# Loading the second experts' weights in 4-MB pairs of units instead of single 2-MB units

## The reference, cut to what matters

```python
def hierarchical_moe(h, w_group, b_group, w_router, b_router, w_gate, w_up, w_down):
    ...
    comb = (jax.nn.one_hot(g_idx[:, 0], N_GROUPS, dtype=jnp.float32)[:, :, None]
            * inner[:, None, :]).astype(h.dtype)
    y = jnp.zeros_like(t)
    for g in range(N_GROUPS):
        a = jnp.einsum('td,edf->tef', t, w_gate[g])
        b = jnp.einsum('td,edf->tef', t, w_up[g])
        hid = jax.nn.silu(a) * b * comb[:, g, :, None]
        y = y + jnp.einsum('tef,efd->td', hid, w_down[g])
    return y.reshape(bsz, seq, d)
```

## Time and profile before

| | |
|---|---|
| time, median of 3 runs (all) | 1499.01 us (1494.44, 1502.03, 1499.01) |
| the profiled execution: its time, its span | 1499.14 us, 1497.3 us |
| PE busy | 1427.2 us, 95% of the span |
| DVE, ACT, POOL busy | 838.1, 571.6, 33.0 us |
| DMA | 443.45 MB, mean 296 GB/s over the span |
| mean granted PE clock | 0.990 |

### The profile page before, as it was taken

One profiled execution on the slowest core, in us unless ns is written; L12 is line 12 of the kernel. 1 busy time (PEld: TensorE's weight loads), 2 busy tenths in 40 slices (PEclk: granted clock), 3 DMA queues, 4 the chain that ended last, 5 costly groups with the idle time before them and its releaser, 6 DMA issues.

```text
span 1497.3 us, 24233 instructions
## 1 busy us (share of the span) xinstructions
PE 1427.2 (95%) x10238; PEld 1004.0 (67%) x10238; DVE 838.1 (56%) x1362; ACT 571.6 (38%) x850; POOL 33.0 (2%) x34
## 2 busy tenths in 40 slices
PE   9999999999999999999899987999999999999897
PEld 9988879999988888873588436984443443443335
DVE  6777697899979679940589207772212112112118
ACT  5673246564543447730477005432111111110115
POOL 0000100000030000000000001000000000000001
PEclk9999999999999999999999999999999999999999
DMA  9441026454531239999999995599999999999991
GB/s 379 158 154 59 2 112 230 158 225 169 184 141 60 85 131 418 406 362 412 412 419 368 420 420 207 198 426 373 427 427 427 426 427 426 427 427 427 426 425 63
DMA packets 48354, 443.45 MB, mean 296 GB/s; under 512 B 6768, under 2 KB 7280, under 8 KB 17008
## 3 DMA queue, kind: packets, MB, share of 16 engines
q1 hardware_dynamic: 47088, 438.37, 72.0%
q10 hardware_dynamic: 1152, 3.46, 0.7%
HBM read 440.75 MB, written 1.05 MB: 295 GB/s over the span
## 4 chain that ended last, share of the span: by engine, by line
PE 73%; DVE 12%; DMA 9%; ACT 3%; issue 2%; PEldq 0%; DVEq 0%; ACTq 0%; SPq 0%; PEld 0%
PE psum L241 71%; DMA sb_spare<-moe_up 3%; DMA sb_work<-moe_up 3%; DMA sb_work<-moe_last 2%; DVE sb_ring_r L1339 2%; DMA sb_ring<-moe_last 1%; DVE sb_work L3100 1%; PE psum L2885 1%; DVE sb_work L1433 0%; DVE sb_ring_r L300 0%; DVE sb_ring_r L2211 0%; DMA sb_ring<-w_dense 0%; PE psum L2289 0%; DVE sb_work L1859 0%; DVE sb_work L1431 0%
## 5 line engine op out<-in xcount | busy, mean ns | idle before, releaser
L241 PE MATMUL psum<-sb_work 128*64 128x512 f32 (+12 forms) x3580 | 330.7, 343 | 21.4 <-DVE sb_work L3100 7.8
L241 PEld LDWEIGHTS psum<-sb_work 128*64 128x64 f32 (+5 forms) x3580 | 168.0, 144 | 159.1 <-issue 135.8
L241 PE MATMUL psum<-sb_ring,sb_work 128*64 128x512 f32 (+2 forms) x660 | 159.3, 600 | 12.0 <-DVE sb_work L3100 4.7
L241 PE MATMUL psum<-sb_xT_r,sb_ring_r 128*128 128x256 f32 x512 | 143.9, 283 | 0.0
L241 PE MATMUL psum<-sb_split 128*128 128x512 f32 (+1 forms) x398 | 128.6, 382 | 0.0
L241 PEld LDWEIGHTS psum<-sb_ring,sb_work 128*64 128x64 f32 (+1 forms) x660 | 51.4, 141 | 104.0 <-issue 97.9
L3098 DVE TENSOR_TENSOR sb_work<-sb_work,psum 128x512 f32<-128x512 f32 x16 | 11.0, 687 | 167.7 <-ACT sb_work L3010 167.7
L3010 ACT ACTIVATE sb_work<-psum 128x512 f32<-128x512 f32 x16 | 9.6, 598 | 240.2 <-PE psum L241 240.2
L241 PEld LDWEIGHTS psum<-sb_xT_r,sb_ring_r 128*128 128x128 f32 x512 | 98.1, 192 | 0.3
L3068 DVE SCALAR_TENSOR_TENSOR sb_out_even<-psum,sb_work,sb_out_even 128x512 fp32r<-128x512 f32 x32 | 22.6, 747 | 125.8 <-ACT sb_out_even L2996 125.8
L241 PE MATMUL psum<-sb_split,sb_lnp_r 128*128 128x512 f32 (+1 forms) x260 | 87.8, 376 | 4.1 <-DVE sb_ring_r L2211 3.7
(11 more groups left out here) (524 smaller groups left out, 2881.6 us busy)
## 6 DMA issues: line engine op xcount, KB each, us to landing
sb_work<-moe_up SPq DMA_DIRECT2D x33, 2048.0 KB, 25.9
sb_ring<-moe_wide SPq DMA_DIRECT2D x52, 1024.0 KB, 10.3
sb_ring<-w_dense SPq DMA_DIRECT2D x23, 2048.0 KB, 8.5
sb_work<-moe_wide SPq DMA_DIRECT2D x43, 1024.0 KB, 11.1
sb_ring<-moe_up SPq DMA_DIRECT2D x18, 2048.0 KB, 25.3
sb_work<-moe_down SPq DMA_DIRECT2D x17, 2048.0 KB, 24.1
sb_ring<-ffn_wide SPq DMA_DIRECT2D x14, 2048.0 KB, 7.4
sb_ring<-moe_down SPq DMA_DIRECT2D x9, 2048.0 KB, 25.3
```

What stands on the lines that cost most here:

```text
L241: return nc.tensor.matmul(o, lhsT, rhs, start=start, stop=stop, **kw)
```

## The change

Two units whose homes are neighbours are loaded by one DMA of 4 MB, 128 rows of 32 KB. Homes 0 and 1, 2 and 3, 4 and 5, 6 and 7 become four such pairs; homes 8 and 9 stay single. Ring slots are given to homes 6 to 8 anew, so that 6 and 7 are slots 0 and 1; home 8 is now the slot that comes free first. `work`'s end and `spare` get one name together, `late_homes`. A pair has one semaphore, PE waits on it for either unit, and SP loads a pair when PE has read the second unit that was in it. In DRAM two units of a pack now lie in one row.

```diff
+        with nc.sbuf_tensor("sb_below_late", [P, EXTRA_AT], F32), \
+                nc.sbuf_tensor("sb_late_homes", [P, 4 * UNIT], F32) as late_homes:
+            pass
...
-        M2_RING = {6: U_MOE2 - 3, 7: U_MOE2 - 2, 8: U_MOE2 - 1}
+        M2_RING = {i: next(u for u in range(U_MOE2 - RING, U_MOE2) if u % RING == i - 6) for i in (6, 7, 8)}
+        PAIRED = 8
...
+        def home2_pair(n):
+
+            i = n % HOMES2
+            if i < 4:
+                return late_homes[:, UNIT * i:UNIT * (i + 2)]
+            if i == 4:
+                return work[:, SPLIT_AT:SPLIT_AT + 2 * UNIT]
+            return ring[:, 0:2, :].rearrange("p a d -> p (a d)")
+
+        def home2_sem(n):
+
+            i = n % HOMES2
+            return i - i % 2 if i < PAIRED else i
...
-                pe.wait_ge(sem(f"home_loaded{n % HOMES2}"), 16 * (m1_home_loads(n % HOMES2) + n // HOMES2 + 1 + (n % HOMES2 == LAST_HOME)))
+                r = home2_sem(n)
+                pe.wait_ge(sem(f"home_loaded{r}"), 16 * (m1_home_loads(r) + n // HOMES2 + 1 + (r == LAST_HOME)))
...
-                src = I["moe2_up"][g, j] if j < UP_UNITS else I["moe2_down"][g, j - UP_UNITS]
+                src = I["moe2_up"][g, j // 2] if j < UP_UNITS else I["moe2_down"][g]
+                if n % HOMES2 < PAIRED:
+                    sp.dma_start(home2_pair(n), src).then_inc(sem(f"home_loaded{home2_sem(n)}"), 16)
+                    return
+                src = src[:, UNIT * (j % 2):UNIT * (j % 2) + UNIT]
...
-                for n in range(4):
+                for n in (0, 2):
                     pack_load(n)
...
-                released(M2_RING[6])
+                released(M2_RING[8])
+                pack_load(8)
+                sp.wait_ge(sem("x_split"), 8 + HALVES)
+                pack_load(4)
+                for n in (6, 7):
+                    released(M2_RING[n])
                 pack_load(6)
-                sp.wait_ge(sem("x_split"), 8 + HALVES)
-                for n in (4, 5):
-                    pack_load(n)
-                for n in (7, 8):
-                    released(M2_RING[n])
-                    pack_load(n)
...
                 for n in range(HOMES2, UNITS2):
-                    unit_read(n - HOMES2)
-                    pack_load(n)
+                    if n % HOMES2 >= PAIRED:
+                        unit_read(n - HOMES2)
+                        pack_load(n)
+                    elif n % 2 == 0:
+                        unit_read(n + 1 - HOMES2)
+                        pack_load(n)
```

More of the change, by code:

```diff
@@ L2765, in program @@
         M2_UNIT_STEP = [f"k{UP_K * i + UP_K - 1}" for i in range(UP_UNITS)] + [f"d{DOWN_C * i + DOWN_C - 1}" for i in range(DOWN_UNITS)]
-        M2_RING = {6: U_MOE2 - 3, 7: U_MOE2 - 2, 8: U_MOE2 - 1}
+        M2_RING = {i: next(u for u in range(U_MOE2 - RING, U_MOE2) if u % RING == i - 6) for i in (6, 7, 8)}
+        PAIRED = 8
         def home2(n):
             i = n % HOMES2
[L2771 to L2774, removed]
+            if i < 4:
+                return late_homes[:, UNIT * i:UNIT * (i + 1)]
             if i == LAST_HOME:
@@ L2779, in home2 @@
             return work[:, SPLIT_AT + UNIT * (i - 4):SPLIT_AT + UNIT * (i - 3)]
-        assert SPLIT_AT + 2 * UNIT <= EXTRA_AT and EXTRA_AT + 3 * UNIT <= WORK
+        assert SPLIT_AT + 2 * UNIT <= EXTRA_AT and EXTRA_AT + 3 * UNIT == WORK
+        def home2_pair(n):
+            i = n % HOMES2
+            if i < 4:
+                return late_homes[:, UNIT * i:UNIT * (i + 2)]
[5 more added lines that the diff above has]
+            return i - i % 2 if i < PAIRED else i
         def m2_pe_names(g):
@@ L3111, in program @@
         OVER_BLOCKS = (FF_BLOCKS, (FF2 // P,), (FF2 // P,))
+        OVER_LOADED = (48, 80, 80)
         OVER_FIRST = (SLOTS1, SLOTS2, SLOTS2 + P)
@@ L3145, in overflow_sync @@
                             for i in range(2):
-                                sp.dma_start(ring[:, i, :].rearrange("p (u r) -> p u r", u=UP_UNITS),
-                                             I["moe2_up"][g].rearrange("u d (e w r) -> d e w u r", e=PACK, w=2)[:, e, i])\
-                                    .then_inc(loaded, 16)
+                                for b in range(2):
+                                    sp.dma_start(ring[:, i, 2 * D * b:2 * D * (b + 1)].rearrange("p (u r) -> p u r", u=2),
+                                                 I["moe2_up"][g, b].rearrange("d (u e w r) -> d e w u r", u=2, e=PACK, w=2)[:, e, i])\
+                                        .then_inc(loaded, 16)
                             sp.dma_start(ring[:, 2, :].rearrange("p (u r) -> p u r", u=DOWN_UNITS),
-                                         I["moe2_down"][g].rearrange("u f (e r) -> f e u r", e=PACK)[:, e])\
+                                         I["moe2_down"][g].rearrange("f (u e r) -> f e u r", u=DOWN_UNITS, e=PACK)[:, e])\
                                 .then_inc(loaded, 16)
@@ L3174, in overflow_body_tensor @@
                     over_wait(pe, n, it, 3 + 6 * b)
-                    pe.wait_ge(sem(f"over_loaded{n}"), it * (48 * nb) + 48 * (b + 1))
+                    pe.wait_ge(sem(f"over_loaded{n}"), it * (OVER_LOADED[n] * nb) + OVER_LOADED[n] * (b + 1))
                     w1, w3 = (ring[:, i, 0:DC * nch * P].rearrange("p (k n) -> p k n", k=DC) for i in range(2))
@@ L4086, in layouts @@
     A["moe2_up"] = gate_up.reshape(PACKS, PACK, UP_UNITS, UP_K, P, 2, FF2).transpose(0, 2, 4, 1, 5, 3, 6)\
-        .reshape(PACKS, UP_UNITS, P, -1)
-    A["moe2_down"] = inp["w_down_2"][0].reshape(PACKS, PACK, DOWN_UNITS, DOWN_C, P, D).transpose(0, 2, 4, 1, 3, 5)\
-        .reshape(PACKS, DOWN_UNITS, P, -1)
+        .reshape(PACKS, UP_UNITS // 2, 2, P, -1).transpose(0, 1, 3, 2, 4).reshape(PACKS, UP_UNITS // 2, P, -1)
+    A["moe2_down"] = inp["w_down_2"][0].reshape(PACKS, PACK, DOWN_UNITS, DOWN_C, P, D).transpose(0, 4, 2, 1, 3, 5)\
+        .reshape(PACKS, P, -1)
     return {k: np.ascontiguousarray(v, dtype=f32) for k, v in A.items()}
```

## The result

| | before | changed |
|---|---|---|
| median (range), 16 runs each | 1498.82 us (1494.44 to 1502.51) | 1502.63 us (1500.09 to 1509.73) |
| ratio changed to before, 95% interval | | 1.0036 [1.0025, 1.0047] |
| profiled execution: time, span | 1499.14, 1497.3 us | 1500.09, 1498.3 us |

The changed kernel is slower. The medians lie 3.8 us apart; the ratio says 0.36%, which is 5.4 us (3.7 to 7.0). The forecast was 1503.4 us, 4.3 us more than before, and called a difference within 0.5% the likeliest.

A forecast was written before the change was run, and what follows sets the result against it. DMA engines were taken as full through the second experts, PE barely slower. Landings gave +3.4 - 3.1 + 3.6 = +3.9 us, PE's line +2.8 + 1.75 = +4.5; taking +4.3, 1499.14 + 4.3 = 1503.4 us, range 1500 to 1506.5.

The forecast's parts named there:

- The later start, 3.43 us: Ahead of unit 10: the first pair waits until PE has read unit 1, so the DMA hole grows by 3.43 us.
- The gain of long rows, 3.1 us: Paired loads of the second experts: rows of 32 KB save a fixed packet cost of 13.6 ns, 3.1 us in all.
- the rival of packets that stay as they are: Paired loads: rows are cut into 16 KB packets or the cost is not per packet; 1506.1 us, chance 20%.
- that of slower rows: Paired loads: reading addresses 32 KB apart lowers the rate, under 426 GB/s; 1512.6 us, chance 7%.
- Fewer stragglers: Paired loads: half as many packets meet fewer single engine delays, 2 to 4 us back; 1499.2 to 1501.4 us, chance 12%.
- A fixed cost of each transfer: Paired loads: a cost between DMAs is halved for 35 pairs; 0.34 us a pair needed for 0.5% faster; chance 3%.
- The tail, 3.6 us: Stage end: both down units start only after the last pair lands, leaving 3.6 us more behind that landing.
- PE's own line, +4.5: PE from about 1340 us: waits for pairs, mainly 80 and 81, +2.8 us, plus a clock fall of 1.75.
- two lines of 3.9 and 4.5: Stage end: landings alone give +3.9 us, PE's waits and clock about +4.5; the later one sets the end.
- The clock falls twice: PE behind the wait for 80 and 81 and at its flag: a clock fall after both; 1505.4 us, chance 8%.
- the +6.3: Upper bound of PE's added time in the second experts, with twice as much loss from the clock's fall.

The follow-up runs named there:

- e1: The changed kernel with units 10 and 11, the first that wait for PE, loaded singly again; ratio to before 1.0026.
- e2: The changed kernel with the last six units, 90 to 95, loaded singly; ratio to before 1.0030.
- e3: The changed kernel with units 80 and 81 loaded singly; ratio to before 1.0027.
- e5: The changed kernel with each pair sent as two 2-MB DMAs with rows of 16 KB at the pair's time; ratio to before 1.0063.
- the second ones: The kernel before and the changed kernel each profiled once more, unedited; from PE's read of unit 1 to the last down matmuls 429.3 and 433.6 us.
- e9: The changed kernel with units 10 and 11 and all from 70 on loaded singly, 24 pairs left; ratio to before 1.0003.

## Why the prediction was right, step by step

**The later start, 3.43 us: right.** The first data of unit 10 moves 2.5 us before PE's read of unit 1 in the kernel before and 0.9 us after it in the changed one. This came once, and e1 takes it away alone. What it was worth at the end is 1.3 to 2.0 us: with it gone, most of the rest is lost again in the next six units.

**The gain of long rows, 3.1 us: right.** A row of 32 KB is one packet, and 12 ns are saved by it; the forecast had 13.6. Counted by packets, the changed kernel is 3.5 us behind before when ten units have been moved and 0.6 when all 86 have: 2.9 us came back. The landing agrees: 425.3 + 3.4 - 2.9 = 425.8, measured 425.7. So the rival of packets that stay as they are falls, and that of slower rows with it (429 to 431 GB/s, not under 427). Fewer stragglers would have brought the landing 2 to 4 us ahead of the forecast's own sum, 425.3 + 3.4 - 3.1 = 425.6; it did not come. A fixed cost of each transfer is there but small: 9 ns on an engine, not the 0.34 us a pair that this rival needed. Its quoted fit of 2.0 us (the Trainium skill, DMA: Bandwidth & Descriptors, Anatomy of one DMA) is one for DMAs issued by GpSimd; the loads here are issued by SP, so this trace does not speak against that fit.

**The tail, 3.6 us: the arithmetic holds, but it is not on the path.** Counted by landings alone the end would be at 425.7 + 7.4 = 433.1; PE ended at 434.3. e2 shows it: single loads at the end change nothing while PE is late from pair 80 and 81. With that wait gone (e3), what binds in the tail is the wait for pair 90 and 91. In no run did PE wait for the last landing (it came closest in e5, where the load landed at 1455.9 and the down units started at 1455.99), so the 3.6 us themselves were never seen.

**PE's own line, +4.5: right in kind, and a little small.** PE waited at unit 66 (1.06, which I had not foreseen), at 72 (0.75 where 1.4 was forecast; its pair landed 0.1 us before the start) and at 74 (0.35). So it came to pair 80 and 81 later, and its wait there was 3.11 us, under the 3.4 to 5.6 forecast. What counts is when it was through with unit 81: 6.6 us later in the stretch than before, of which 1.7 are the slow spell (1.75 forecast) and 4.9 the pair's landing, where 4.3 were forecast. Later waits that fell away took back 1.4 (1.5 forecast). That makes +5.2. The first executions of the two kernels differ by 5.2, the second ones by 4.3. I had put 4.3 between two lines of 3.9 and 4.5; since the later line sets the end, the sum should have been 4.5 or a little more. That 4.3 lies between the 3.8 of the medians and the 5.4 of the ratio is in part luck: the terms are each off by up to 0.7 us.

**A rival that was priced wrong.** "The clock falls twice" happened by its words: the changed kernel has a slow spell behind the wait for 80 and 81 and one at the flag. But the one at the flag is in the time before as well, so it adds nothing, and the +6.3 counted it a second time.

**Smaller slips.** The windows before do not all stop at 427 GB/s: one of 5 us shows 433. 1503.4 less 4 is 1499.4, not 1499.2, and 0.34 us is 7% of a unit's step, not 6%. And the 12 ns could have been read before the change: that trace has packets of 8192 bytes too, with a median of 313 ns, and twice 313 less 614 is 12.

What stays open is when idle time of 2.4 to 3 us costs a slow spell and when not; in the runs here both happened.

## What to carry to other kernels

When loads run back to back at full rate, all that the longer rows saved here was the fixed part of their packets, 0.8% of the paired loads. What pairs cost is set elsewhere: a home is free only when both units in it are read, and data is there only when both have landed, each one unit later. Look at how many loaded units the consumer still has in hand along the stage; where that is under two, as here in the last third, pairing turns into waits. And take such edits away in groups: two waits that cover one another were each worth nothing alone here. Count the slow spells of the clock in both traces before you credit a difference of 2 us to an edit.

## What I had not expected

The moment at which PE has read unit 1 differs by 9.6 us between the eleven profiled executions of this case (1024.09 in e9 to 1033.67 in e3), though these two load the first ten units in the same way, while the stretch behind it repeats to 0.2 and 0.7 us where the same kernel ran twice. Behind the stretch all eleven take 38.1 or 38.2 us, so most of the scatter of the whole time lies ahead of the stage. A difference of 1 us in one stage is read from the trace, not from the times.
